# A 31-tap depthwise filter split into two phases, its gate taken from PSUM on VectorE, and a bias added as a matrix product

## The chip, the cores and the metric

One core of one Trainium2 chip. The metric is the time of one execution on the device in microseconds (us), the median over runs. The profile is one further execution, recorded by the hardware profiler; engines are TensorE (PE, its weight loads PEld), VectorE (DVE), ScalarE (ACT), GpSimd (POOL) and SyncE (SP, which here only issues DMAs).

## The reference

A backbone trunk with two layers over 1280 tokens (256 of context, 1024 latent) of 1024 channels. The first layer's mixer is a convolution module, and the change lies there:

```python
def conv_module(h, pw1_w, pw1_b, dw_w, dw_b, ln_g, ln_b, pw2_w, pw2_b):
    a, g = jnp.split(h @ pw1_w + pw1_b, 2, axis=-1)
    u = a * jax.nn.sigmoid(g)
    u = lax.conv_general_dilated(u, dw_w[:, None, :], window_strides=(1,),
                                 padding=[(CONV_PAD, CONV_PAD)], ...,
                                 feature_group_count=d) + dw_b      # 31 taps for each channel
    u = jax.nn.silu(layernorm(u, ln_g, ln_b))
    return u @ pw2_w + pw2_b
```

Context and latent tokens are filtered apart, each with zeros around it. Every sub-layer is modulated by rows of `silu(c) @ ada_w + ada_b` (6 x 1024 columns for each layer, for two vectors c). After the mixer come a mixture of experts, then a gated linear attention layer and a second mixture of experts. All of it is fp32.

## The kernel before

The program is a row of stages with a barrier between them. The stage of the change is `conv_taps`. It goes over the 1024 output channels in 8 chunks of 128 (channels on partitions, tokens along the columns).

Every fp32 product is made of three: weights and activations are split into a high half (`hi`, fp32r) and what is left (`lo`), and `product3` adds hi x hi, hi x lo, lo x hi. For each chunk SyncE loads the weights of both halves of `pw1` (`raw`, two buffers), ScalarE makes the high half (L577), GpSimd the low half (L477, 128 x 2048). TensorE makes three groups of tokens (0: 256 context tokens, 1 and 2: 512 latent tokens each) into PSUM: `zg` for the gate and `za` for the value, 48 matmuls for each group. ScalarE writes sigmoid(zg + bias) to `sg` (L601) and za + bias to `u` (L603); GpSimd multiplies them in place (L485). `u` has two buffers with zero columns between context and latent tokens.

VectorE then makes the 31 taps of the chunk over all 1295 columns: two scalar multiplies (L646, L648), 29 fused multiply-adds alternating between two accumulators (L653), and one sum of the two (L657) into `vt`, which the next stage reads. Before a chunk it copies that chunk's column of taps and biases to `vec` (L628). ScalarE's sigmoids of chunk n wait until the taps of chunk n-2 are summed.

In the same stage TensorE works off 20 units of modulation rows: 2 x 512 columns each, 64 matmuls with two stationary columns, in four strips of the array (L554). A unit's weights are two loads of 1 MB (`ada_w`), one buffer each, so a load waits until TensorE has used the half before it. There are five units for two chunks: three behind the even chunk, two behind the odd one. ScalarE takes the sums from PSUM (L588), GpSimd adds the bias, which SyncE has loaded (L498), and stores the two rows (L502).

Waits are written by hand with semaphores; the loops over pairs of chunks are hardware loops, with the first pair (and VectorE's last) written out.

Of the kernel before, what the change touches and what calls it, by code (L numbers as in the profile page):

```python
# [5 lines left out]
F32 = mybir.dt.float32  # L6
# [4 lines left out]
ALU = mybir.AluOpType  # L11
# [3 lines left out]
P = 128  # L15
# [373 lines left out]
STRIP = 32  # L389


def conv_taps(nc, d, ht, vt, vecs, cs):
# [3 lines left out]
    with ExitStack() as ctx:  # L396
# [5 lines left out]
        ada_b = ph.sb("ada_b", [P, P])  # L402
        ada_sum = ph.sb("ada_sum", [P, P])
        ada_row = ph.sb("ada_row", [P, P])
# [3 lines left out]
        vec = [ph.sb(f"vec{b}", [P, VEC_ROWS]) for b in range(2)]  # L408
        sg = [ph.sb(f"sg{g}", [P, N]) for g in range(3)]
        u = [ph.sb(f"u{b}", [P, CONV_W]) for b in range(2)]  # L410
        acc = [ph.sb(f"acc{b}", [P, CONV_OUT]) for b in range(2)]
# [3 lines left out]
        pairs = KC // 2  # L415

        with nc.Block() as block:
            @block.sync
            def _(sp):
                sp.dma_start(ident[:, :], d.ident).then_inc(s("rows_loaded"), 16)  # L420
                for r0, src in ((0, d.dw_w), (V_DWB, d.dw_b), (V_LNG, d.ln_g), (V_LNB, d.ln_b)):
                    n = src.shape[0]
                    sp.dma_start(rows[r0:r0 + n, :], src).then_inc(s("rows_loaded"), 16)
                sp.dma_start(rows[V_BA:V_BG + 1, :], d.pw1_b.rearrange("o (h n) -> (o h) n", h=2))\
                    .then_inc(s("rows_loaded"), 16)

                def load(b, i):
                    for h in range(2):
                        src = d.pw1_w[:, ds((i * 2 + b) * P + h * D, P)].rearrange("(k p) n -> p k n", p=P)
                        sp.dma_start(raw[b][:, :, h, :], src).then_inc(s(f"w_loaded{b}"), 16)  # L430

                def load_unit(j, i, first):
                    _, l, per, at, c0 = ADA_UNITS[j]
                    u = i * len(ADA_UNITS) + j
                    col = (i * per + at) * N + c0
                    for h in range(2):
                        if not (first and j == 0):

                            sp.wait_ge(s(f"ada_used{h}"), u)
                        half = slice(h * (KC // 2), (h + 1) * (KC // 2))  # L440
                        sp.dma_start(ada_w[h][:, :, :], d.ada_w[l, :, ds(col, N)]
                                     .rearrange("(p k) n -> p k n", k=KC)[:, half, :]).then_inc(s(f"ada_loaded{h}"), 16)
                    if not (first and j == 0):
                        sp.wait_ge(s("ada_out"), u)
                    else:
                        sp.wait_ge(s("ada_b_zero"), 1)
                    for st in (LAT, CTX):
                        sp.dma_start(ada_b[st:st + 3 * STRIP + 1:STRIP, :],
                                     d.ada_b[l, ds(col, N)].rearrange("(j n) -> j n", n=P))\
                            .then_inc(s("ada_b_loaded"), 16)  # L450

                def pair(i, first, last):
                    for b in range(2):
                        for j, unit in enumerate(ADA_UNITS):
                            if unit[0] == b:
                                load_unit(j, i, first)
                        if not last:

                            sp.wait_ge(s(f"w_lo{b}"), i + 1)
                            load(b, i + 1)  # L460

                for b in range(2):
                    load(b, 0)
                pair(0, True, False)
                with sp.Fori(1, pairs - 1) as i:
                    pair(i, False, False)
                pair(pairs - 1, False, True)

            @block.gpsimd
            def _(pool):  # L470
                pool.memset(ada_b[:, :], 0.0).then_inc(s("ada_b_zero"), 1)
                for b in range(2):
                    pool.memset(u[b][:, :], 0.0).then_inc(s("u_zero"), 1)

                def low(b, i):
                    pool.wait_ge(s(f"w_hi{b}"), i + 1)
                    pool.tensor_tensor(w.lo[:, :, :, :], raw[b][:, :, :, :], w.hi[:, :, :, :].bitcast(F32),  # L477
                                       ALU.subtract).then_inc(s(f"w_lo{b}"), 1)

                def gate(b, i):  # L480

                    for g, (t0, n, c0) in enumerate(CONV_GROUPS):
                        pool.wait_ge(s(f"sig_ready{g}{b}"), i + 1)
                        pool.wait_ge(s(f"a_ready{g}{b}"), i + 1)
                        pool.tensor_tensor(u[b][:, c0:c0 + n], u[b][:, c0:c0 + n], sg[g][:, 0:n], ALU.mult)\  # L485
                            .then_inc(s(f"u_ready{g}{b}"), 1)

                def units_out(b, i, first):

                    for j, (when, l, per, at, c0) in enumerate(ADA_UNITS):  # L490
                        if when != b:
                            continue
                        u = i * len(ADA_UNITS) + j
                        pool.wait_ge(s("ada_b_loaded"), (u + 1) * 32)
                        pool.wait_ge(s("ada_taken"), u + 1)
                        if not (first and j == 0):
                            pool.wait_ge(s("stored"), u * 32)
                        pool.tensor_tensor(ada_row[:, :], ada_sum[:, :], ada_b[:, :], ALU.add)\  # L498
                            .then_inc(s("ada_out"), 1)
                        pool.wait_ge(s("ada_out"), u + 1)  # L500
                        for st in (LAT, CTX):
                            pool.dma_start(d.mods[l].rearrange("s m n -> s (m n)")[st, ds((i * per + at) * N + c0, N)]  # L502
                                           .rearrange("(j n) -> j n", n=P),
                                           ada_row[st:st + 3 * STRIP + 1:STRIP, :]).then_inc(s("stored"), 16)

                low(0, 0)
                gate(0, 0)
                low(1, 0)
                units_out(0, 0, True)
                gate(1, 0)  # L510
                with pool.Fori(1, pairs) as i:
                    low(0, i)
                    units_out(1, i - 1, False)
                    gate(0, i)
                    low(1, i)
                    units_out(0, i, False)
                    gate(1, i)
                units_out(1, pairs - 1, False)
                pool.wait_ge(s("stored"), 32 * pairs * len(ADA_UNITS))

            @block.tensor
            def _(pe):
                pe.wait_ge(s("rows_loaded"), 96)
                pe.wait_ge(s("ada_acc_zero"), 1)
# [4 lines left out]
                def chunk(b, i, first):  # L529
                    pe.wait_ge(s(f"w_lo{b}"), i + 1)  # L530
                    for g, (t0, n, _) in enumerate(CONV_GROUPS):

                        if not (first and b == 0):
                            pe.wait_ge(s(f"a_ready{g}{1 - b}"), i + b)
                        for h, z in ((1, zg[g]), (0, za[g])):
                            for k in range(KC):
                                last = product3(pe, z[:, 0:n], w.hi[:, k, h, :], w.lo[:, k, h, :],
                                                ht.hi[:, k, t0:t0 + n], ht.lo[:, k, t0:t0 + n], k == 0, k == KC - 1)
                        last.then_inc(s(f"z_ready{g}{b}"), 1)

                def units(b, i, first):
                    for j, unit in enumerate(ADA_UNITS):
                        if unit[0] != b:
                            continue
                        u = i * len(ADA_UNITS) + j
                        if not (first and j == 0):

                            pe.wait_ge(s("ada_taken"), u)
                        for h in range(2):
                            pe.wait_ge(s(f"ada_loaded{h}"), (u + 1) * 16)  # L550
                            for k in range(KC // 2):
                                for j4 in range(N // P):

                                    last = pe.matmul(ada_acc[j4 * STRIP:j4 * STRIP + 2, 0:P],  # L554
                                                     cs[:, h * (KC // 2) + k, :], ada_w[h][:, k, j4 * P:(j4 + 1) * P],
                                                     start=h == 0 and k == 0, stop=h == 1 and k == KC // 2 - 1)
                            last.then_inc(s(f"ada_used{h}"), 1)

                for b in range(2):
# [2035 lines left out]
```

## Time and profile before

| | |
|---|---|
| Median of 3 runs | 3328.24 us (3327.05 to 3329.19) |
| Profiled execution | 3323.5 us, span 3321.9 us |
| Granted TensorE clock, mean | 0.867 of full speed |
| Filter stage | 118.2 to 588.5 us of the span |
| VectorE's taps | 169.39 to 588.45 us, 8 chunks |

The span is from the first to the last instruction. An engine's busy time leaves waiting out. A line such as L653 is a line of the kernel; an operation made in a loop or a helper has one line for all its instances. In a timeline, consecutive instructions of one line stand merged as one row with their count, so the row's duration is that of all of them.

### The profile page before, as it was taken

How to read it: one execution, taken by the hardware profiler on the slowest of the kernel's cores; microseconds unless marked ns; L12 is line 12 of the kernel's file. 1: busy time of each engine (PE TensorE's matmuls, PEld its weight loads, DVE VectorE, ACT ScalarE, POOL GpSimd, SP SyncE). 2: the span in 40 equal slices, each digit the busy share in tenths (PEclk: the TensorE clock that was granted, in tenths of full speed). 3: DMA queues.
4: the chain of work that ended last, by engine and by line, in shares of the span. 5: the costliest groups of instructions: out<-in, count | busy, mean ns of one | idle time of the engine just before them, and what ended most of it. 6: DMA issues, size and time to landing. Idle time of an engine off the chain costs nothing. (4 is left out here: it accounts for less than half of the span.)

```text
span 3321.9 us, 40914 instructions
## 1 busy us (share of the span) xinstructions
PE 2565.6 (77%) x13098; PEld 2050.7 (62%) x13098; DVE 2097.9 (63%) x1722; ACT 1406.0 (42%) x1455; POOL 512.9 (15%) x499
## 2 busy tenths in 40 slices
PE   4587770595399999999933998978494499999980
PEld 1466660484278888888832886757473388888860
DVE  2399999455476767588526001338554588888865
ACT  0211110443166666577523112434322277777752
POOL 0133320100000010001033000045200101001004
PEclk7688885796599999999965999989796699999995
DMA  8244330224188889799654211013454499999965
GB/s 301 92 153 153 126 107 20 96 76 172 42 322 311 322 320 327 280 349 385 264 219 172 100 48 52 20 53 109 172 194 147 153 376 382 393 383 391 394 254 215
DMA packets 297755, 701.18 MB, mean 211 GB/s; under 512 B 22640, under 2 KB 50096, under 8 KB 297654
## 3 DMA queue, kind: packets, MB, share of 16 engines
q1 hardware_dynamic: 259082, 570.79, 47.5%
q0 software_dynamic: 22656, 75.60, 6.4%
q10 hardware_dynamic: 15936, 53.75, 4.3%
q8 instruction: 47, 0.77, 0.1%
q14 instruction: 34, 0.28, 0.0%
HBM read 610.05 MB, written 91.06 MB: 211 GB/s over the span
## 5 line engine op out<-in xcount | busy, mean ns | idle before, releaser
L1394 DVE TENSOR_TENSOR moe_w_lo<-moe_w_raw,moe_w_hi 128x2048 fp32r<-128x2048 f32 x384 | 862.0, 2286 | 83.8 <-ACT moe_w_hi L1323 48.7
L1323 ACT ACTIVATE moe_w_hi<-moe_w_raw 128x2048 fp32r<-128x2048 f32 x384 | 714.8, 1909 | 63.9 <-issue 37.6
L653 DVE SCALAR_TENSOR_TENSOR taps_acc<-taps_u,taps_vec,taps_acc 128x1295 f32<-128x1295 f32 x232 | 387.2, 1744 | 0.0
L98 PE MATMUL moe_pg<-moe_w_hi,moe_xt_hi 128*128 128x512 f32 x592 | 243.8, 412 | 11.2 <-DVE moe_xt_lo L1405 5.9
L98 PE MATMUL moe_py<-moe_w_hi,moe_at_hi 128*128 128x512 f32 x592 | 241.6, 408 | 11.9 <-DVE moe_w_lo L1394 8.2
L99 PE MATMUL moe_pg<-moe_w_lo,moe_xt_hi 128*128 128x512 f32 x592 | 237.0, 400 | 0.0
L100 PE MATMUL moe_pg<-moe_w_hi,moe_xt_lo 128*128 128x512 f32 x592 | 236.8, 400 | 0.0
L99 PE MATMUL moe_py<-moe_w_lo,moe_at_hi 128*128 128x512 f32 x592 | 235.2, 397 | 0.0
L100 PE MATMUL moe_py<-moe_w_hi,moe_at_lo 128*128 128x512 f32 x592 | 234.8, 397 | 0.0
L100 PE MATMUL moe_pu<-moe_w_hi,moe_xt_lo 128*128 128x512 f32 x592 | 234.3, 396 | 0.0
L98 PE MATMUL moe_pu<-moe_w_hi,moe_xt_hi 128*128 128x512 f32 x592 | 234.1, 396 | 0.0
L99 PE MATMUL moe_pu<-moe_w_lo,moe_xt_hi 128*128 128x512 f32 x592 | 234.1, 396 | 0.0
L1226 POOL COPY moe_idx<-plan_token 128x1 int32 (+1 forms) x76 | 16.0, 210 | 1076.6 <-PE moe_pxt L1264 1076.5
L1440 DVE TENSOR_TENSOR moe_a<-moe_sil,moe_pu 128x512 f32<-128x512 f32 x74 | 50.9, 688 | 180.5 <-issue 130.4
L364 PE MATMUL norm_pt<-norm_ident,norm_h 128*128 128x128 f32 x224 | 55.1, 427 | 119.3 <-DVE norm_h L334 119.3
L1333 ACT ACTIVATE moe_y<-moe_py 128x1024 f32<-128x1024 f32 x74 | 76.0, 1027 | 146.1 <-PE moe_py L100 146.1
L98 PEld LDWEIGHTS moe_pg<-moe_w_hi,moe_xt_hi 128*128 128x128 f32 x592 | 113.4, 192 | 36.3 <-issue 12.4
L98 PEld LDWEIGHTS moe_py<-moe_w_hi,moe_at_hi 128*128 128x128 f32 x592 | 112.2, 190 | 35.8 <-issue 12.3
L1232 POOL DMA_INDIRECT moe_xg<-scratch_experts_in,moe_idx x76 | 115.0, 1514 | 123.4 <-issue 123.4
L1348 ACT ACTIVATE moe_xt_hi<-moe_pxt 128x1024 fp32r<-128x1024 f32 x74 | 75.8, 1024 | 129.4 <-PE moe_pxt L1264 129.4
L98 PE MATMUL glav_acc<-glav_w_hi,ht_next_hi 128*128 128x512 f32 x288 | 114.9, 399 | 20.0 <-DVE glav_w_lo L1738 20.0
L100 PEld LDWEIGHTS moe_pg<-moe_w_hi,moe_xt_lo 128*128 128x128 f32 x592 | 113.2, 191 | 27.4
(305 smaller groups left out, 5366.0 us busy)
## 6 DMA issues: line engine op xcount, KB each, us to landing
moe_w_raw<-in_moe_w SPq DMA_DIRECT2D x384, 1024.0 KB, 12.6
taps_ada_w<-in_ada_w SPq DMA_DIRECT2D x40, 1024.0 KB, 7.0
scratch_experts_out<-moe_y ACTq DMA_DIRECT2D x57, 512.0 KB, 6.4
norm_x<-scratch_residual SPq DMA_DIRECT2D x28, 512.0 KB, 3.3
scan_v<-scratch_gla_values SPq DMA_DIRECT2D x20, 512.0 KB, 4.0
scratch_experts_in<-norm_h POOLq DMA_DIRECT2D x18, 512.0 KB, 3.0
comb_x<-scratch_residual SPq DMA_DIRECT2D x18, 512.0 KB, 6.9
ada_w<-in_ada_w SPq DMA_DIRECT2D x4, 2048.0 KB, 28.0
```

The source lines that it names most:

```text
L98: pe.matmul(out, xh, wh, start=start, stop=False)
L99: pe.matmul(out, xh, wl, start=False, stop=False)
L100: return pe.matmul(out, xl, wh, start=False, stop=stop)
L364: last = pe.transpose(pt[b][:, k, :], h[b][:, k * P:(k + 1) * P], ident[:, :])
L653: dve.scalar_tensor_tensor(acc[q][:, :], u[b][:, k:k + CONV_OUT], vec[b][:, k:k + 1], acc[q][:, :], ALU.mult, ALU.add).then_inc(s(f"tap{q} ...
L1226: pool.tensor_copy(idx[:, :], plan.token[:, ds(k, 1)]).then_inc(s("idx_ready"), 1)
L1232: pool.indirect_dma_start(xg[0:rows, :], None, d.hd[:, :], bass.IndirectOffsetOnAxis(idx[0:rows, :], 0))\
L1323: act.activation(hi[m][:, cut, :], raw[m][p][:, cut, :], ACT.Copy).then_inc(s(f"{m}_hi{h}"), 1)
L1333: act.activation(y[:, :], py[:, :], ACT.Copy).then_inc(s("y_out"), 1)
L1348: act.activation(xt_hi[:, :, :], pxt[:, :, :], ACT.Copy).then_inc(s("xt_hi"), 1)
L1394: dve.tensor_tensor(lo[m][:, cut, :], raw[m][p][:, cut, :], hi[m][:, cut, :].bitcast(F32), ALU.subtract).then_inc(s(f"{m}_lo{h}"), 1)
L1440: dve.tensor_tensor(a[:, :], sil[:, :], pu[:, :], ALU.mult).then_inc(s("a_ready"), 1)
```

## The change

- **Filter.** The padded columns of `u` are stored as two phases (even and odd columns, 664 each; the zero columns become 16 and 32, so that both phases start alike, and the output has 1298 columns). With u0, u1 the phases and w the taps, one sum is shared: S = sum over j of (w[2j] + w[2j+1]) u1[j], 16 half-length taps. The even outputs are S + sum of w[2j] (u0 - u1)[j], 16 taps on `back`; the odd outputs are S + sum of w[2j+1] (u0 shifted by one - u1)[j], 15 taps on `ahead`. So 47 taps of 649 columns take the place of 31 of 1295, and there are two subtractions and two joins, which write every second column of `vt`. The summed taps (`both`) are made once.
- **Gate.** VectorE reads `za` from PSUM and does (za + bias) * sg in one instruction for each group, writing the two phases. ScalarE's L603 and GpSimd's L485 go. Gate n+1 stands on VectorE between the even and the odd half of chunk n. TensorE's groups of the next chunk wait for it (`u_ready`), since `za` and `zg` have one buffer for each group.
- **Modulation bias.** Four matmuls with one row (`one` x `ada_b`) start each unit's sums; GpSimd's L498 and `ada_sum` go, ScalarE writes one of five `ada_row` buffers, and GpSimd only issues the stores.
- **Order.** Units stand behind single groups (after groups 0, 1, 2 in even chunks, after 1 and 2 in odd ones; the first chunk keeps all three behind group 2). GpSimd makes the low half of chunk n+1 ahead of the stores of chunk n's units. The per-chunk vector copies go. The hardware loops over pairs become plain written-out code.

```diff
-GAP = PAD + CTX_LEN + PAD
-CONV_GROUPS = [(0, CTX_LEN, PAD), (CTX_LEN, N, GAP), (CTX_LEN + N, N, GAP + N)]
-CONV_W = GAP + SEQ + PAD
-CONV_OUT = GAP + SEQ - PAD
+LEAD = PAD + 1
+GAP = LEAD + CTX_LEN + LEAD
+CONV_GROUPS = [(0, CTX_LEN, LEAD), (CTX_LEN, N, GAP), (CTX_LEN + N, N, GAP + N)]
+CONV_W = GAP + SEQ + LEAD
+CONV_OUT = CONV_W - 2 * PAD
...
+EVEN, ODD = (TAPS + 1) // 2, TAPS // 2
+HALF_OUT = CONV_OUT // 2
...
+        def units_behind(n, g):
+            units = units_of(n)
+            if n == 0:
+                return units if g == 2 else []
+            return units[g:g + 1] if len(units) == 3 else units[g - 1:g] if g else []
...
             @block.gpsimd
+                low(0)
+                for n in range(KC):
+                    if n + 1 < KC:
+                        low(n + 1)
+                    for at in units_of(n):
...
+                        pool.wait_ge(s("ada_taken"), at + 1)
                         for st in (LAT, CTX):
+                            pool.dma_start(..., ada_row[j][st:st + 3 * STRIP + 1:STRIP, :]).then_inc(s(f"stored{j}"), 16)
...
             @block.tensor
+                def unit(at):
...
+                    for j4 in range(N // P):
+                        pe.matmul(ada_acc[j4 * STRIP:j4 * STRIP + 2, 0:P], one[:, :], ada_b[:, j4 * P:(j4 + 1) * P],
+                                  start=True, stop=False)
...
+                for n in range(KC):
+                    pe.wait_ge(s("w_lo"), n + 1)
+                    for g, (t0, m, _) in enumerate(CONV_GROUPS):
+                        if n:
+                            pe.wait_ge(s(f"sig_ready{g}"), n)
+                            pe.wait_ge(s(f"u_ready{g}"), n)
                         for h, z in ((1, zg[g]), (0, za[g])):
...
+                        last.then_inc(s(f"z_ready{g}"), 1)
+                        for at in units_behind(n, g):
+                            unit(at)
...
             @block.scalar
+                        act.activation(sg[g][:, 0:m], zg[g][:, 0:m], ACT.Sigmoid, bias=vecs[:, n, V_BG:V_BG + 1])\
+                            .then_inc(s(f"sig_ready{g}"), 1)
+                        if g == 2 and n + 1 < KC:
+                            high(n + 1)
+                        for at in units_behind(n, g):
+                            take(at)
...
             @block.vector
+                def gate(n):
+                    for g, (t0, m, c0) in enumerate(CONV_GROUPS):
+                        dve.wait_ge(s(f"z_ready{g}"), n + 1)
+                        dve.wait_ge(s(f"sig_ready{g}"), n + 1)
+                        dve.scalar_tensor_tensor(
+                            u[n % 2][:, :, c0 // 2:(c0 + m) // 2].rearrange("p q m -> p m q"),
+                            za[g][:, 0:m].rearrange("p (m q) -> p m q", q=2), vecs[:, n, V_BA:V_BA + 1],
+                            sg[g][:, 0:m].rearrange("p (m q) -> p m q", q=2), ALU.add, ALU.mult)\
+                            .then_inc(s(f"u_ready{g}"), 1)
...
+                gate(0)
+                for n in range(KC):
+                    for g in range(3):
+                        dve.wait_ge(s(f"u_ready{g}"), n + 1)
+                    if n:
+                        dve.wait_ge(s("odd_done"), n)
+                    dve.tensor_tensor(back[:, :], u[n % 2][:, 0, :], u[n % 2][:, 1, :], ALU.subtract)\
+                        .then_inc(s("back"), 1)
+                    shared(n, 0)
+                    dve.tensor_tensor(ahead[:, :], u[n % 2][:, 0, 1:], u[n % 2][:, 1, 0:CONV_W // 2 - 1], ALU.subtract)\
+                        .then_inc(s("ahead"), 1)
+                    even(n, 0)
+                    for j in range(1, EVEN):
+                        shared(n, j)
+                        even(n, j)
+                    join(n, 0, "even_done", 0)
+                    if n + 1 < KC:
+                        gate(n + 1)
+                    dve.wait_ge(s("even_done"), n + 1)
+                    for j in range(ODD):
+                        odd(n, j)
+                    join(n, 1, "odd_done", 1)
```

`shared`, `even` and `odd` are one instruction each: a scalar multiply where they begin a sum (shared 0, even 0 with the filter's bias, odd 1 with the bias), otherwise a fused multiply-add into one of the two accumulators, after a wait for the one before on that accumulator. `join` waits for both and adds them into every second column of `vt`.

## Rows read from the trace of the kernel before

**Rows 1.** The page, busy us of an engine, share of the span, instructions.

```profile
PE 2565.6 (77%) x13098; PEld 2050.7 (62%) x13098; DVE 2097.9 (63%) x1722; ACT 1406.0 (42%) x1455; POOL 512.9 (15%) x499
```

**Rows 2.** Windows: length, busy PE, PEld, DVE, ACT, POOL, clock, DMA share, GB/s.

```profile
276.00:330.00 54.00, 47.69 (x372) 39.99 (x373) 53.97 (x34) 5.89 (x10) 19.87 (x13) 0.86 0.46 153
...
545.00:592.00 47.00, 0.00 (x0) 0.00 (x0) 43.47 (x31) 0.00 (x0) 0.00 (x0) 0.50 0.01 4
```

**Rows 3.** Waits, 118 to 592 us: who waited for whom, total, times, longest.

```profile
ACT taps_sg L601 <- DVE taps_vec L628: 90.1, 4, 30.4
...
PE taps_ada_acc L554 <- DMA taps_ada_w<-in_ada_w: 70.7, 23, 10.9
DVE taps_acc L646 <- POOL taps_u L485: 39.9, 1, 39.9
```

**Rows 4.** Timeline of VectorE: start, duration, line, operation, tiles, count.

```profile
169.39 0.95 DVE L646 TENSOR_SCALAR taps_acc<-taps_u,taps_vec 128x1295 f32<-128x1295 f32 x1 [39.91 <-POOL taps_u L485]
...
335.26 49.90 DVE L653 SCALAR_TENSOR_TENSOR taps_acc<-taps_u,taps_vec,taps_acc 128x1295 f32<-128x1295 f32 x29
...
542.28 0.95 DVE L646 TENSOR_SCALAR taps_acc<-taps_u,taps_vec 128x1295 f32<-128x1295 f32 x1
543.15 0.89 DVE L648 TENSOR_SCALAR taps_acc<-taps_u,taps_vec 128x1295 f32<-128x1295 f32 x1
543.96 42.95 DVE L653 SCALAR_TENSOR_TENSOR taps_acc<-taps_u,taps_vec,taps_acc 128x1295 f32<-128x1295 f32 x29
586.94 1.51 DVE L657 TENSOR_TENSOR taps_out<-taps_acc 128x1295 f32<-128x1295 f32 x1
```

**Rows 5.** Groups of VectorE by line and shape: busy us, mean ns, idle before.

```profile
L653 DVE SCALAR_TENSOR_TENSOR taps_acc<-taps_u,taps_vec,taps_acc 128x1295 f32<-128x1295 f32 x29 | 42.9, 1559 | 0.0
...
L2258 DVE SCALAR_TENSOR_TENSOR scan_state<-scan_state,scan_fall,scan_pds 128x256 f32<-128x256 f32 x80 | 33.2, 476 | 45.7 <-PE scan_pds L2113 45.7
...
L991 DVE COPY route_lg<-route_pt 128x256 f32<-128x256 f32 x1 | 0.4, 424 | 0.0
```

**Rows 6.** Timeline of VectorE in the attention scan, four fused operations.

```profile
2226.94 1.64 DVE L2258 SCALAR_TENSOR_TENSOR scan_state<-scan_state,scan_fall,scan_pds 128x256 f32<-128x256 f32 x4
```

**Rows 7.** Timeline of GpSimd and VectorE where a low half meets taps.

```profile
350.79 5.76 POOL L477 TENSOR_TENSOR taps_w_lo<-taps_raw,taps_w_hi 128x2048 fp32r<-128x2048 f32 x1
...
401.88 5.09 POOL L477 TENSOR_TENSOR taps_w_lo<-taps_raw,taps_w_hi 128x2048 fp32r<-128x2048 f32 x1 [0.64 <-ACT taps_w_hi L577]
...
402.53 5.81 DVE L653 SCALAR_TENSOR_TENSOR taps_acc<-taps_u,taps_vec,taps_acc 128x1295 f32<-128x1295 f32 x1
```

**Rows 8.** Timeline of ScalarE, chunks 0 and 1; a sigmoid starts when its group ends.

```profile
166.75 0.69 ACT L601 ACTIVATE taps_sg<-taps_zg,taps_vec 128x512 f32<-128x512 f32 x1 [9.61 <-PE taps_za L100]
...
167.90 1.91 ACT L577 ACTIVATE taps_w_hi<-taps_raw 128x2048 fp32r<-128x2048 f32 x1
169.70 0.28 ACT L588 ACTIVATE taps_ada_sum<-taps_ada_acc 128x128 f32<-128x128 f32 x1
...
186.69 0.28 ACT L588 ACTIVATE taps_ada_sum<-taps_ada_acc 128x128 f32<-128x128 f32 x1 [8.80 <-PE taps_ada_acc L554]
193.47 0.48 ACT L601 ACTIVATE taps_sg<-taps_zg,taps_vec 128x256 f32<-128x256 f32 x1 [6.50 <-PE taps_za L100]
...
204.33 0.69 ACT L601 ACTIVATE taps_sg<-taps_zg,taps_vec 128x512 f32<-128x512 f32 x1 [10.02 <-PE taps_za L100]
```

**Rows 9.** Windows around a group of 512 columns and around two units.

```profile
193.00:204.30 11.30, 11.30 (x53) 9.41 (x52) 11.30 (x8) 0.84 (x2) 1.25 (x1) 1.00 0.07 24
...
169.70:177.50 7.80, 3.73 (x64) 2.04 (x64) 7.80 (x4) 0.28 (x2) 7.18 (x4) 0.61 0.67 245
...
398.80:402.00 3.20, 1.77 (x64) 1.42 (x56) 3.20 (x3) 3.17 (x4) 1.21 (x2) 1.00 0.26 65
```

**Rows 10.** DMA issues of the page: count, KB each, median us to landing.

```profile
taps_ada_w<-in_ada_w SPq DMA_DIRECT2D x40, 1024.0 KB, 7.0
```

More of the change, by code:

```diff
@@ L401, in conv_taps @@
         ada_w = [ph.sb(f"ada_w{h}", [P, KC // 2, N]) for h in range(2)]
-        ada_b = ph.sb("ada_b", [P, P])
-        ada_sum = ph.sb("ada_sum", [P, P])
-        ada_row = ph.sb("ada_row", [P, P])
+        ada_b = ph.sb("ada_b", [1, N])
+        one = ph.sb("one", [1, 2])
+        ada_row = [ph.sb(f"ada_row{j}", [P, P]) for j in range(len(ADA_UNITS))]
         ada_acc = ph.ps("ada_acc", [P, N])
@@ L452, in pair @@
[L452 to L466, printed above, removed]
@@ L467, in _ @@
-                pair(pairs - 1, False, True)
+                        if h == 0:
+                            sp.dma_start(ada_b[:, :], d.ada_b[layer:layer + 1, col:col + N])\
+                                .then_inc(s("ada_b_loaded"), 16)
+                for n in range(2):
+                    load(n)
+                for n in range(KC):
+                    for at in units_of(n):
+                        load_unit(at)
+                    if n + 2 < KC:
+                        load(n + 2)
@@ L480, in gate @@
[L480 to L500, printed above, removed]
+                    pool.memset(u[b][:, :, :], 0.0).then_inc(s("u_zero"), 1)
@@ L508, in _ @@
[L508 to L519, printed above, removed]
+                                           ada_row[j][st:st + 3 * STRIP + 1:STRIP, :]).then_inc(s(f"stored{j}"), 16)
@@ L521, in _ @@
+                for j in range(per_pair):
+                    pool.wait_ge(s(f"stored{j}"), 32 * (total // per_pair))
             @block.tensor
@@ L539, in chunk @@
[L539 to L557, printed above, removed]
@@ L559, in _ @@
-                for b in range(2):
-                    chunk(b, 0, True)
-                    units(b, 0, True)
-                with pe.Fori(1, pairs) as i:
-                    for b in range(2):
-                        chunk(b, i, False)
-                        units(b, i, False)
+                                last = product3(pe, z[:, 0:m], w.hi[:, k, h, :], w.lo[:, k, h, :],
+                                                ht.hi[:, k, t0:t0 + m], ht.lo[:, k, t0:t0 + m], k == 0, k == KC - 1)
@@ L660, in _ @@
-                vector(0, 0)
-                for b in range(2):
-                    chunk(b, 0, first=True)
-                with dve.Fori(1, pairs - 1) as i:
-                    for b in range(2):
-                        chunk(b, i)
-                for b in range(2):
-                    chunk(b, pairs - 1, last=True)
-                dve.wait_ge(s("taps_summed"), KC)
+                dve.tensor_tensor(both[:, :, 0:ODD], vecs[:, :, 0:2 * ODD:2], vecs[:, :, 1:2 * ODD:2], ALU.add)\
+                    .then_inc(s("both_ready"), 1)
```

213 lines of the change are left out of this document (106 added, 107 removed).

## The prediction

> **What bounds the kernel now.** The page comes first: over the whole span VectorE is busy 63% and TensorE 77% [rows 1]. These are averages over stages with different limits; the edit lies in one stage, the filter stage, from 118.2 to 588.5 us. So I cut that stretch into windows [rows 2]. VectorE is busy through the whole of the middle window and nearly all of the last, while TensorE, at 47.69 of 54 us in the middle, does nothing in the last: the taps set the end. The waits of the stage say the same from the other side [rows 3]: the sigmoids wait 90.1 us for VectorE (through the vector copy), VectorE itself waits once, 39.9 us, at the start, for the first gated chunk. TensorE's 70.7 us of waiting for modulation weights is hidden behind VectorE, but it must be kept in mind for a change that makes VectorE quicker.
>
> Then the timeline of VectorE [rows 4]. Taps run from 169.39 to 586.94 + 1.51 = 588.45 us, 419.1 us for 8 chunks. The last chunk has GpSimd idle: 29 fused taps in 42.95 us, so one every 1.481 us. Its duration is 1559 ns for 1295 columns and that of the fused operation of 256 columns 476 ns [rows 5]: 1083 / 1039 = 1.042 ns a column. 1295 columns are then 1.349 us, and 0.132 us of the spacing is fixed. A chunk with GpSimd at work takes 49.90 us for the same 29: 6.95 us lost.
>
> **The new VectorE chunk.** Half a chunk's output is 649 columns. I need the fixed part at a short length: four fused operations of 256 take 1.64 us in all with 0.476 for the last [rows 5, 6], so one starts every 0.388 us, 0.267 of it elements and 0.121 fixed. The fixed part doesn't shrink with length. I take 0.13: 0.676 + 0.13 = 0.806 us per fused half-length tap.
> - Even half: 30 fused taps 24.2; two scalar multiplies, which go at two elements per cycle (1295 start to start in 0.81, of which 0.675 are elements [rows 4]), 0.47 and 0.54; two subtractions of 664 and 663 at 0.77; the join 0.76 (its row is 1.51 for 1295 [rows 4], 0.16 fixed, less 0.08 of overlap with the next); 0.3 where an operation waits for the one just before it. Sum 27.8 us.
> - Odd half: 14 fused 11.3, one scalar multiply 0.54, join 0.76, 0.2 for waits: 12.8 us.
> - Gate, new on VectorE: 256 + 512 + 512 columns out of PSUM, 1.33 + 3 x 0.13 = 1.7 us. The 256-column row reads PSUM too and has no extra [rows 5].
>
> Taps are then 40.6 us a chunk against 46.2 before (542.28 to 588.45). A quarter of the multiplications goes (47 x 649 against 31 x 1295 elements), an eighth of the time, because 31 fixed parts and one join become 51 and more.
>
> **GpSimd.** A fused tap has two SBUF inputs. The one that met a low half took 5.81 us where 1.56 is usual [rows 7]: 4.25 us lost, for a low half of 5.09 us in all. That stays, 7 times. The gates and bias sums on GpSimd go; with them 6.95 - 4.25 = 2.7 us a chunk. The gate on VectorE has one SBUF input. The Trainium skill's page "SBUF — State Buffer", section "Who interferes with whom", calls this an exclusive lock held for the whole instruction, against VectorE operations with two SBUF inputs. The row of 5.81 agrees, and by that rule the new gate would be free of it; my sum puts no loss on it either way.
>
> So a steady chunk is 27.8 + 1.7 + 12.8 + 4.25 = 46.6 us; before, 46.2 + 7.0 = 53.2 (the chunk of the 49.90).
>
> **The new wait.** VectorE runs in order, and gate(n+1) stands between the halves of chunk n. In chunk 0 it comes too early. Chunk 0's third group ends at 166.75 as now [rows 8]; sigmoid and gate bring VectorE's start to 168.1 (169.39 before, since the identity pass on ScalarE and GpSimd's multiply are gone). Even half plus the low half of chunk 1: 168.1 + 27.8 + 4.25 = 200.2. TensorE still makes three modulation units back to back behind chunk 0, limited by their 1 MB loads (7.0 us each [rows 10]), to 186.7; then group 0 by 193.5, group 1 by 204.3 [rows 8]. Now one unit stands before group 2: 1.77 us of matmul at clock 1.00 [rows 9], and 0.1 for its four bias products. Group 2, 10.9 us like group 1, ends at 217.2, sigmoid 217.9, gate 218.6. VectorE stands for about 17 us, and behind it the odd half.
>
> From there: 218.6 + 12.8 + 6 x 46.6 + 40.6 = 551.6 us. The stage ends 36.9 us earlier. Other edits I cost at nothing: the bias load and products (TensorE has spare time), 8 vector copies of 0.2 on VectorE that go (inside the 0.3s), two small operations on the summed taps (VectorE idle before 168), the unrolled loops. Without TensorE's cover the bias products would be 20 x 0.1 = 2 us. The stores of the modulation rows stay on GpSimd's queue behind the next low half; the row they wait for is in its own buffer, and only the unit five later needs it.
>
> **Does TensorE keep up?** Chunk n+2 may start when gate(n+1) has read PSUM and the low half is there: sigmoid 0.7, high half 1.9, low half up to 5.8 after group 2 [rows 7, 8], 8.4 us. Groups take 7, 10.9 and 10.9 (group 0 has half the columns of group 1 and yet took 193.47 - 186.69 = 6.8 us: it starts at the lower clock), units inside 1.9 each [rows 8, 9]. With two inside that is 8.4 + 28.8 + 3.8 = 41.0 us from group 2 to group 2. 41.0 is below 46.6. Released by the gate instead, it delivers 0.4 + 28.8 + 3.8 + 0.7 = 33.7 us after it. At gate(2): VectorE gets there at 218.6 + 12.8 + 27.8 + 4.25 = 263.5; TensorE has it at 217.2 + 41.0 + 0.7 = 258.9. A unit's two loads, 7 us each and overlapping, lie behind a group of 10.9 us, or behind the wait for the low half.
>
> **Strided places.** The gate writes the two phases alternately, the joins every second column. The nearest row is the reordering copy with a source step of 8 columns: 424 ns for 256 [rows 5], which is 0.267 of elements and the same 0.16 fixed as the join. I take no extra; the other bound is double time for the five operations of a chunk, 2.7 us. The Trainium skill ("Advanced Engine Details and Errata", "SBUF Cachelines") speaks against the change here: full rate wants two hits on a 16-byte line, and the gate's alternating writes have none in a row. By it the time would be rival C's; the reordering copy's row doesn't bear it out, but that one reads PSUM.
>
> **Rivals.**
> - A, the forecast: VectorE bounds after one stall. 0.71. Its own range 3284 to 3307: fixed part between 0.12 and 0.16 for some 55 operations in each of 8 chunks (-4 to +13 us), the stall 14 to 19 us.
> - B, units keep waiting for loads inside a chunk (8.5 us each, as (186.69 - 169.70) / 2 now). Three-unit chunks then need 8.4 + 28.8 + 17 = 54.2 us from group 2 to group 2. Gate 2 is 8.6 us late (217.2 + 54.2 + 0.7 against 263.5), gates 4 and 6 each 54.2 + 45.7 - 2 x 46.6 = 6.7: +22, 3313. For it: 70.7 us of waits now. Against: now they are back to back. 0.11.
> - C, strided writes at half rate: 8 x 1.35 for joins and 6 x 1.33 for gates, +19: 3310. 0.10.
> - D, the slower side: TensorE's clock. It now pauses in each chunk and runs thin unit matmuls between groups; the granted clock was 0.61 in a unit that waited for its weights [rows 9]. If it stayed at the lower level (1.2 GHz) for all of the groups, 28.8 becomes some 55 and the loop 67 us: 6 x 20 us lost, 3413. It decides against the change from a loop of 46.6 + 37/6 = 52.8 us. Against: group 1 runs at 1.00 behind a group 0 that starts low [rows 9]. 0.04.
> - Better than A (low halves falling into VectorE's waits, 4.25 us each, three or four times): 3275. 0.04.
>
> **Numbers.** The profiled execution took 3323.5 us, its span 3321.9; the median of the three is 3328.24, 0.14% more. The difference is taken from the median: 3328.2 - 36.9 = 3291.3. The range must leave out D and part of the tails: 3279 to 3313. A measurement tells about 0.2%, 7 us. Faster: A, B, C and the better case, 0.94; within: 0.02; slower: 0.04.
>
> **What would show it.** The half-length fused tap: duration near 0.88 us, one per 0.806. The first chunk: VectorE idle 17 us before a gate, and no long wait at later gates. One tap a chunk stretched by 4.2 us. TensorE waits for the gates, not the other way round. Taps end near 552. The prediction is wrong if the wait before gates repeats (B or D), if gate or join durations are twice their element time (C), or if the fixed part grows with the two chains now one tap of 0.8 us apart.

## The result and the profile after

| | before | after |
|---|---|---|
| Median of 4 runs | 3328.72 us (3327.05 to 3330.28) | 3291.57 us (3288.28 to 3293.28) |
| Profiled execution | 3323.5 us, span 3321.9 | 3288.3 us, span 3286.7 |
| Granted TensorE clock, mean | 0.867 | 0.876 |
| Filter stage | 118.24 to 588.45, 470.2 us | 120.39 to 554.38, 434.0 us |

The ratio is 0.989 (0.9877 to 0.9902): the changed kernel is 37 us faster, and 3291.3 was forecast. The filter stage is 36.2 us shorter; the forecast had 36.9.

The page first, which answers to [rows 1]: busy time of each engine over the span.

```profile
PE 2559.9 (78%) x13258; PEld 2053.7 (62%) x13258; DVE 2053.0 (62%) x1892; ACT 1393.6 (42%) x1431; POOL 462.6 (14%) x455
```

It says little, as before. The stage says more. Groups of the stage by line and form (count | busy us, mean ns of one | idle before and what ended it):

```profile
L614 DVE SCALAR_TENSOR_TENSOR taps_acc<-taps_back,channel_vectors,taps_acc 128x649 f32<-128x649 f32 x120 | 107.0, 892 | 0.0
L602 DVE SCALAR_TENSOR_TENSOR taps_acc<-taps_u,taps_both,taps_acc 128x649 f32<-128x649 f32 x120 | 107.0, 891 | 0.0
L629 DVE SCALAR_TENSOR_TENSOR taps_acc<-taps_ahead,channel_vectors,taps_acc 128x649 f32<-128x649 f32 x112 | 91.4, 890 | 0.0
...
L484 POOL TENSOR_TENSOR taps_w_lo<-taps_raw,taps_w_hi 128x2048 fp32r<-128x2048 f32 x8 | 58.0, 7255 | 248.0 <-ACT taps_w_hi L552 248.0
...
L636 DVE TENSOR_TENSOR taps_out<-taps_acc 128x649 f32<-128x649 f32 x16 | 33.9, 2118 | 1.1
...
L589 DVE SCALAR_TENSOR_TENSOR taps_u<-taps_za,channel_vectors,taps_sg 128x512 f32<-128x512 f32 x16 | 16.8, 1112 | 33.8 <-ACT taps_sg L567 33.8
...
L589 DVE SCALAR_TENSOR_TENSOR taps_u<-taps_za,channel_vectors,taps_sg 128x256 f32<-128x256 f32 x8 | 5.2, 656 | 15.6 <-ACT taps_sg L567 15.6
```

Three things are to be seen. The half-length tap takes 890 ns whatever it reads, as forecast (0.88). The gate's 512 columns take 1112 ns. And GpSimd's low half, 5.09 us in [rows 7], is 7.3 us on average.

VectorE's timeline of one steady chunk and of the last one (start, us for the row; rows of several instructions are merged):

```profile
237.42 0.84 DVE L650 TENSOR_TENSOR taps_ahead<-taps_u 128x663 f32<-128x663 f32 x1
238.18 0.61 DVE L610 TENSOR_SCALAR taps_acc<-taps_back,channel_vectors 128x649 f32<-128x649 f32 x1
238.71 0.89 DVE L602 SCALAR_TENSOR_TENSOR taps_acc<-taps_u,taps_both,taps_acc 128x649 f32<-128x649 f32 x1
239.51 0.89 DVE L614 SCALAR_TENSOR_TENSOR taps_acc<-taps_back,channel_vectors,taps_acc 128x649 f32<-128x649 f32 x1
...
262.06 0.89 DVE L614 SCALAR_TENSOR_TENSOR taps_acc<-taps_back,channel_vectors,taps_acc 128x649 f32<-128x649 f32 x1
263.06 4.94 DVE L636 TENSOR_TENSOR taps_out<-taps_acc 128x649 f32<-128x649 f32 x1
267.91 2.55 DVE L589 SCALAR_TENSOR_TENSOR taps_u<-taps_za,channel_vectors,taps_sg 128x256 f32<-128x256 f32 x3
270.30 0.87 DVE L629 SCALAR_TENSOR_TENSOR taps_acc<-taps_ahead,channel_vectors,taps_acc 128x649 f32<-128x649 f32 x1
...
283.16 0.85 DVE L647 TENSOR_TENSOR taps_back<-taps_u 128x664 f32<-128x664 f32 x1
...
310.02 4.94 DVE L636 TENSOR_TENSOR taps_out<-taps_acc 128x649 f32<-128x649 f32 x1
...
513.90 0.85 DVE L647 TENSOR_TENSOR taps_back<-taps_u 128x664 f32<-128x664 f32 x1
...
553.55 0.83 DVE L636 TENSOR_TENSOR taps_out<-taps_acc 128x649 f32<-128x649 f32 x1
```

Thirty fused taps start from 238.71 to 262.06, one every 0.805 us. From join to join it is 310.02 - 263.06 = 46.96 us (46.6 forecast). The stretched instruction is the join, not a tap: 4.94 us against 0.83. The last chunk runs from 513.90 to 554.38, 40.5 us (40.6 forecast). In the kernel before, the chunks between the first and the last two take 53.3 us on average (227.00 to 493.53 for five); this is 47.0 in their place.

GpSimd's low halves in the same view:

```profile
219.87 4.48 POOL L484 TENSOR_TENSOR taps_w_lo<-taps_raw,taps_w_hi 128x2048 fp32r<-128x2048 f32 x1 [30.97 <-ACT taps_w_hi L552]
261.09 6.21 POOL L484 TENSOR_TENSOR taps_w_lo<-taps_raw,taps_w_hi 128x2048 fp32r<-128x2048 f32 x1 [34.51 <-ACT taps_w_hi L552]
303.01 11.26 POOL L484 TENSOR_TENSOR taps_w_lo<-taps_raw,taps_w_hi 128x2048 fp32r<-128x2048 f32 x1 [32.37 <-ACT taps_w_hi L552]
```

Each of the last two ends 0.7 us before the stretched join does (267.30 against 268.00, 314.27 against 314.96). The third began 303.01, 7.0 us before the join of 310.02, and VectorE's taps in between went at their usual spacing: GpSimd stood, and VectorE lost nothing until the join.

The wait in chunk 0, on VectorE:

```profile
201.77 0.84 DVE L636 TENSOR_TENSOR taps_out<-taps_acc 128x649 f32<-128x649 f32 x1
202.52 0.69 DVE L589 SCALAR_TENSOR_TENSOR taps_u<-taps_za,channel_vectors,taps_sg 128x256 f32<-128x256 f32 x1
204.80 1.13 DVE L589 SCALAR_TENSOR_TENSOR taps_u<-taps_za,channel_vectors,taps_sg 128x512 f32<-128x512 f32 x1 [1.59 <-ACT taps_sg L567]
218.08 1.17 DVE L589 SCALAR_TENSOR_TENSOR taps_u<-taps_za,channel_vectors,taps_sg 128x512 f32<-128x512 f32 x1 [12.15 <-ACT taps_sg L567]
219.08 0.87 DVE L629 SCALAR_TENSOR_TENSOR taps_acc<-taps_ahead,channel_vectors,taps_acc 128x649 f32<-128x649 f32 x1
```

From 202.52 to 219.08 VectorE does 3 us of gates and stands for 13.7 us. Later gates have no wait: three in 2.55 us at 267.91. The waits of the stage confirm it (us in total, times, longest):

```profile
PE taps_zg L99 <- DVE taps_u L589: 53.5, 5, 13.1
DVE taps_u L589 <- ACT taps_sg L567: 49.4, 5, 15.6
```

TensorE now waits for the gates, up to 13.1 us at a time. VectorE's 49.4 us are these 13.7 and the wait for the very first groups.

### The profile page after: what moved, and what is told of

It is laid out like the page before. It is cut to its first block and busy times, and to the rows that moved or that the text cites. A ratio compares the mean times of both kernels' runs of the same rounds, so it can differ in the third digit from the quotient of the medians.

```text
span 3286.7 us, 41009 instructions
## 1 busy us (share of the span) xinstructions
PE 2559.9 (78%) x13258; PEld 2053.7 (62%) x13258; DVE 2053.0 (62%) x1892; ACT 1393.6 (42%) x1431; POOL 462.6 (14%) x455
## 5 line engine op out<-in xcount | busy, mean ns | idle before, releaser
L567 ACT ACTIVATE taps_sg<-taps_zg,channel_vectors 128x512 f32<-128x512 f32 (+1 forms) x24 | 14.8, 616 | 290.6 <-PE taps_za L101 290.6
```

Of the source, the lines that this page charges most:

```text
L567: act.activation(sg[g][:, 0:m], zg[g][:, 0:m], ACT.Sigmoid, bias=vecs[:, n, V_BG:V_BG + 1])\
```

## Experiments

The ratios are against the kernel before, run on the same chip. The changed kernel's own ratio, 0.989, is the other mark. The length of the filter stage in the one profiled execution stands beside them (before 470.2 us, changed 434.0); the time outside the stage was 2850 to 2859 us in the ten profiles, so the stage tells small differences better than the medians do.

**The filter alone.** The kernel before with nothing but the two-phase filter (VectorE's loop over pairs of chunks is written out with it); the phases are read in place out of `u` with a step of 2, and gates, bias sums, units and low halves stay where they were.

```diff
+                    src, tap = u[n % 2][:, 1 + 2 * j:1 + 2 * j + 2 * HALF_OUT - 1:2], both[:, n, j:j + 1]
...
+                    dve.tensor_tensor(back[:, :], u[b][:, 0:CONV_W:2], u[b][:, 1:CONV_W:2], ALU.subtract)\
+                        .then_inc(s("back"), 1)
```

> The kernel before with the two-phase filter alone: gate, low halves, bias and units as before, VectorE reads u in place with a step of two columns. Theory (the halved taps are the gain): VectorE's chunk is 40.6 us of taps plus the 6.95 us that GpSimd took before, 47.5 us; the first chunk starts at the old 169.4 and there is no wait in chunk 0, so the taps end near 540 and the time is 3279 to 3283 us, 8 to 12 below the changed kernel. Rival (GpSimd is held off): in the changed kernel's trace the low half took up to 11.3 us from start to end, because it got the port only at a join; here three gates and a low half of every chunk have to get in between the short taps, the gated chunk comes late, VectorE waits for it, and the time is 3295 to 3312 us. Rival (stepped reads are slow): a tap of the shared sum takes over 1.2 us instead of 0.89, and the time is over 3330 us.

Measured: 3282.93 us, ratio 0.987 (0.9854 to 0.9887), 8.6 us below the changed kernel (7 by the two ratios, whose intervals overlap), and inside the expected 3279 to 3283. The stage is 428.1 us, 5.9 shorter than in the changed kernel. The filter makes all of the gain, and what was added to it gains nothing or takes some back. Its taps by line, then GpSimd's and VectorE's operations in the timeline:

```profile
L646 DVE SCALAR_TENSOR_TENSOR taps_acc<-taps_u,taps_both,taps_acc 128x649 f32<-128x649 f32 x120 | 106.5, 888 | 0.0
```

```profile
277.63 20.98 POOL L504 TENSOR_TENSOR taps_ada_row<-taps_ada_sum,taps_ada_b 128x128 f32<-128x128 f32 x1 [5.98 <-ACT taps_ada_sum L594]
...
308.16 6.24 POOL L491 TENSOR_TENSOR taps_u<-taps_u,taps_sg 128x512 f32<-128x512 f32 x1 [5.73 <-ACT taps_u L609]
314.36 5.10 POOL L483 TENSOR_TENSOR taps_w_lo<-taps_raw,taps_w_hi 128x2048 fp32r<-128x2048 f32 x1
...
371.15 0.88 POOL L504 TENSOR_TENSOR taps_ada_row<-taps_ada_sum,taps_ada_b 128x128 f32<-128x128 f32 x1 [5.14 <-ACT taps_ada_sum L594]
```

```profile
298.40 0.91 DVE L680 TENSOR_TENSOR taps_out<-taps_acc 128x649 f32<-128x649 f32 x1
...
313.30 1.79 DVE L680 TENSOR_TENSOR taps_out<-taps_acc 128x649 f32<-128x649 f32 x1
315.01 4.49 DVE L638 COPY taps_vec<-channel_vectors 128x36 f32<-128x36 f32 x1
```

The taps of L646 read with a step of 2 and take 888 ns, no more than contiguous ones. GpSimd's gate of 512 columns is held as well (1.09 us in the kernel before at 400.15, 6.24 here), until VectorE's join at 313.30; the low half behind it then goes straight through, and VectorE's small copy (0.18 us elsewhere) takes 4.49 beside it. The longest wait is that of a bias sum of 128 columns, 0.5 us of work: 20.98 us, until the join at 298.40.

**The rest alone.** The changed kernel with 31 full-length taps; gate n+1 stands behind tap 20 of chunk n.

```diff
-                    dve.tensor_tensor(back[:, :], u[n % 2][:, 0, :], u[n % 2][:, 1, :], ALU.subtract)\
-                        .then_inc(s("back"), 1)
...
+                    for k in range(TAPS):
+                        if k == CUT and n + 1 < KC:
+                            gate(n + 1)
+                        tap(n, k)
```

> The changed kernel with the 31 full-length taps back (gate from PSUM on VectorE after tap 20, bias as a product, units between groups, all kept). Theory: taps 46.2 us a chunk, gate 1.7 us as its writes are contiguous here, low half 4.25 us, and a wait of about 16 us in chunk 0; the taps then end some 7 us later than in the kernel before, 3336 us: the rest of the change alone loses. Rival: taking the gates off GpSimd and the units apart is worth its 2.7 us a chunk and more, 3310 us, so that the filter is only half of the gain.

Measured: 3331.43 us, ratio 1.0008 (0.9998 to 1.0017): no difference (stage 471.0 us against 470.2). My 3336 was 5 us too high, the rival's 3310 falls. VectorE and GpSimd in a steady chunk:

```profile
323.15 1.79 DVE L583 SCALAR_TENSOR_TENSOR taps_u<-taps_za,channel_vectors,taps_sg 128x256 f32<-128x256 f32 x3
324.86 5.58 DVE L600 SCALAR_TENSOR_TENSOR taps_acc<-taps_u,channel_vectors,taps_acc 128x1298 f32<-128x1298 f32 x2
```

```profile
311.71 15.89 POOL L481 TENSOR_TENSOR taps_w_lo<-taps_raw,taps_w_hi 128x2048 fp32r<-128x2048 f32 x1 [31.41 <-ACT taps_w_hi L549]
```

The low half is held from 311.71 until the gates at 323.15. It ends 4.45 us after they begin, so part of it lies beside the gates, which it does not slow: they take 1.79 us with this contiguous write. Two taps then take 5.58 where 3.04 is usual, 2.5 us lost instead of 4.25. The chunk is 343.81 - 293.16 = 50.65 us from join to join, against 53.3. Five such chunks save 13.3 us, and chunk 6 (48.1 us against 48.75) 0.6; chunk 0, with 3.13 + 12.54 us of idle, takes 72.5 us (171.66 to 244.16) against 57.6 (169.39 to 227.00), 14.9 more, and eats all of it. The run holds the gate on VectorE, the bias as a product and the order of the units together; no run takes one of them alone.

**The gate's write.** The gate writes each phase contiguously and reads its inputs with a step of 2.

```diff
-                            u[n % 2][:, :, c0 // 2:(c0 + m) // 2].rearrange("p q m -> p m q"),
-                            za[g][:, 0:m].rearrange("p (m q) -> p m q", q=2), vecs[:, n, V_BA:V_BA + 1],
-                            sg[g][:, 0:m].rearrange("p (m q) -> p m q", q=2), ALU.add, ALU.mult)\
+                            u[n % 2][:, :, c0 // 2:(c0 + m) // 2],
+                            za[g][:, 0:m].rearrange("p (m q) -> p q m", q=2), vecs[:, n, V_BA:V_BA + 1],
+                            sg[g][:, 0:m].rearrange("p (m q) -> p q m", q=2), ALU.add, ALU.mult)\
```

> The changed kernel with the gate going phase by phase: it writes each phase contiguously and reads PSUM and the sigmoid with a step of two. In the changed kernel the gate of 512 columns takes 1.14 us where a fused operation of that size would take 0.74, and a join that writes with a step of two takes no extra. Theory (the alternating writes cost it): 0.74 and 0.48 us, three gates 1.7 instead of 2.4 us, 4 to 5 us less in all: 3287 us. Rival (it is the read of PSUM beside a read of SBUF at this width, or the stepped read costs the same): durations stay at 1.1 us, 3291.6 us; if stepped PSUM reads are slower still, above it.

Measured: 3290.72 us, ratio 0.9887 (0.987 to 0.9903). The gate falls from 1112 to 740 ns (512 columns) and from 656 to 474 (256), and the steady chunk from 46.96 to 46.3 us. The stage is 3.8 us shorter in the profiled execution (430.2), while the medians differ by 0.9, less than runs can tell. With full-length taps, where the gate reads and writes contiguously, it takes 0.75 us for 512 columns too, so neither the read of PSUM nor its step of 2 costs anything. So the alternating write is the cause of the longer gate; its effect on the time is too small to be shown by the medians.

**Units from chunk 1 on.** No modulation unit behind chunk 0, one behind each group from chunk 1 until all 20 are done.

```diff
-            units = units_of(n)
-            if n == 0:
-                return units if g == 2 else []
-            return units[g:g + 1] if len(units) == 3 else units[g - 1:g] if g else []
+            at = (n - 1) * 3 + g
+            return [at] if 0 <= at < total else []
```

> The changed kernel with no modulation unit behind chunk 0 and one behind every group from chunk 1 on (20 units over 21 places). Theory: group 2 of chunk 1 is ready near 209 instead of 217.3, VectorE's wait in chunk 0 is 8 to 9 us shorter and nothing else waits, since TensorE needs 41 to 43 us from chunk to chunk and VectorE 47: 3283 us. Rival: with three units in every chunk TensorE becomes the bound (loads of 2 MB behind a group of 256 columns): VectorE waits at later gates and the time is 3291 us or more.

Measured: 3284.86 us, ratio 0.9876 (0.9859 to 0.9892), 6.7 below the changed kernel (stage 428.6 us, 5.4 shorter). VectorE's gates of chunk 0:

```profile
203.55 1.64 DVE L586 SCALAR_TENSOR_TENSOR taps_u<-taps_za,channel_vectors,taps_sg 128x256 f32<-128x256 f32 x2
212.72 1.18 DVE L586 SCALAR_TENSOR_TENSOR taps_u<-taps_za,channel_vectors,taps_sg 128x512 f32<-128x512 f32 x1 [7.53 <-ACT taps_sg L564]
```

The wait is 7.5 us instead of 13.7, and no later gate waits. Six of the 13.7 us come from the units behind chunk 0. What is left is the time TensorE takes for the three groups and the two units now between them. I had expected 8 to 9 us: group 0 of chunk 1, for which TensorE now waits idle until the low half is there, took 8.3 us at a granted clock of 0.68, where it took 5.9 at 1.00 in the changed kernel's profile.

**All units behind group 2.** The other order, with the loads' waits in one place.

```diff
-            if n == 0:
-                return units if g == 2 else []
-            return units[g:g + 1] if len(units) == 3 else units[g - 1:g] if g else []
+            return units if g == 2 else []
```

> The changed kernel with all units of a chunk behind its last group, as in the kernel before. Their weights are then waited for, 8 to 9 us each, and three units take some 19 us behind group 2. Theory: from group 2 to group 2 TensorE needs 19 + 28.8 = 48 us behind a three-unit chunk and 40 behind a two-unit one, but it is ready 9 us before VectorE asks, so the slack takes it: 3289 to 3292 us, as the changed kernel. Rival (the interleaving carries part of the gain): VectorE waits for group 2 at three or more gates, 3300 us or more.

Measured: 3291.72 us, ratio 0.9891 (0.9875 to 0.9908), stage 435.1 us, as the changed kernel. TensorE's waits for DMAs:

```profile
PE taps_ada_acc L515 <- DMA taps_ada_b<-in_ada_b: 40.2, 12, 4.2
...
PE taps_ada_acc L522 <- DMA taps_ada_w<-in_ada_w: 14.1, 12, 2.4
```

TensorE waits 54 us for loads here and loses nothing, because VectorE still sets the pace. Interleaving the units buys nothing in this kernel. It does take the waits away: in the changed kernel TensorE waits 8.0 us for loads in all, the whole of it behind chunk 0, where rival B needed 8.5 us at each unit.

**Low halves on VectorE.** GpSimd makes none; VectorE does, one instruction in the odd half of each chunk up to the sixth, and two ahead of them (the first before any gate, the second among the even taps of chunk 0).

```diff
+                        if j == 1 and n + 2 < KC:
+                            low(n + 2)
                         odd(n, j)
```

> The changed kernel with the low halves of the weights made by VectorE (one operation of 128 x 2048, 2.29 us elsewhere in the trace) in place of GpSimd, which then only issues stores. In the changed kernel each low half on GpSimd stretches one join from 0.84 to 4.94 us. Theory (VectorE pays for GpSimd's work by being locked out, and longer than its own operation takes): 4.1 - 2.2 = 1.9 us for each of 6 low halves behind the first wait, and 2.2 us at the start of the first chunk, together some 13 us: 3277 to 3280 us. Rival (VectorE is the bound and any work added to it is a loss): 15 us more, 3306 us. Second rival: TensorE gets the weights too late and the gates wait, 3290 us.

Measured: 3277.12 us, ratio 0.9847 (0.9831 to 0.9863), 14.5 below the changed kernel (stage 424.1 us, 9.9 shorter).

```profile
259.69 0.83 DVE L633 TENSOR_TENSOR taps_out<-taps_acc 128x649 f32<-128x649 f32 x1
260.44 2.50 DVE L581 SCALAR_TENSOR_TENSOR taps_u<-taps_za,channel_vectors,taps_sg 128x256 f32<-128x256 f32 x3
...
263.57 2.29 DVE L626 TENSOR_TENSOR taps_w_lo<-taps_raw,taps_w_hi 128x2048 fp32r<-128x2048 f32 x1
```

The join is back at 0.83 us. The low half costs VectorE 2.29 us as its own instruction (2.20 until the next one starts, at 265.77) and 4.1 as GpSimd's neighbour. In the profile five chunks of 45.0 us instead of 47.0 and 2.0 us in the odd half of chunk 0 make 11.7 us; gate(1) ended 1.8 us later, counted from the stage's start, behind a group 0 of chunk 1 that took 7.7 us at a granted clock of 0.74. The 2.2 us that I expected at the first chunk bring nothing, since VectorE stands for TensorE at gate(1) (18.4 us here). What the medians show beyond the stage's 9.9 us lies outside the stage and is not explained.

**All three together.** Low halves on VectorE, units from chunk 1 on, contiguous gate write.

> The changed kernel with three edits: low halves on VectorE, no units behind chunk 0 and one behind every group after it, the gate phase by phase. Theory: the gains add, 13 + 7 + 4 us, since VectorE still needs 44.5 us a chunk and TensorE 41 to 43: 3266 to 3270 us. Rival: with VectorE at 44.5 us TensorE's loop becomes the bound in part of the chunks, 3273 to 3280 us.

Measured: 3268.17 us (3265.77 to 3270.60), ratio 0.9818 (0.9802 to 0.9834), stage 410.7 us. The chunk is 298.17 - 253.75 = 44.4 us from join to join. This version is 23 us (0.7%) below the changed kernel and 60 us below the one before; it beats both. Whether low halves on VectorE would do as much for the filter alone, no run shows.

**GpSimd's low half beside the gates.** It stays on GpSimd, but waits for the first gate of the chunk, so that it overlaps instructions that it does not block.

```diff
                     pool.wait_ge(s("w_hi"), n + 1)
+                    if n:
+                        pool.wait_ge(s("u_ready0"), n)
```

> The changed kernel with one more wait: GpSimd starts the low half of chunk n+1 only when VectorE has done group 0 of gate n. The gate has one SBUF input, the taps have two. In the run with full-length taps the low halves began during a gate and a steady chunk lost only 2.5 us to each (50.65 against 48.1 us), where the changed kernel loses 4.1. Theory (only operations with two SBUF inputs are locked out): the low half runs beside groups 1 and 2 of the gate, some 1.8 us of it cost nothing, and the rest is taken from the first odd tap: no join of 4.94 us, an odd tap stretched by 2.3 to 2.8 us instead, six chunks 1.3 to 1.8 us shorter each, 3280 to 3284 us. Rival (the gate is locked out as well, or the low half doesn't get in between the groups): the stretched operation is a gate or again a join, and the time stays at 3291.6 us.

Measured: 3288.12 us, ratio 0.988 (0.9864 to 0.9897); 3.5 below the changed kernel, less than the medians can tell, and above my range. What is shown here is shown by the rows. VectorE, then GpSimd, at one gate:

```profile
264.83 0.83 DVE L638 TENSOR_TENSOR taps_out<-taps_acc 128x649 f32<-128x649 f32 x1
265.58 2.49 DVE L591 SCALAR_TENSOR_TENSOR taps_u<-taps_za,channel_vectors,taps_sg 128x256 f32<-128x256 f32 x3
267.92 3.66 DVE L631 SCALAR_TENSOR_TENSOR taps_acc<-taps_ahead,channel_vectors,taps_acc 128x649 f32<-128x649 f32 x1
```

```profile
266.39 4.50 POOL L486 TENSOR_TENSOR taps_w_lo<-taps_raw,taps_w_hi 128x2048 fp32r<-128x2048 f32 x1 [38.02 <-DVE taps_u L591]
312.00 4.50 POOL L486 TENSOR_TENSOR taps_w_lo<-taps_raw,taps_w_hi 128x2048 fp32r<-128x2048 f32 x1 [37.55 <-DVE taps_u L591]
```

The mechanism is there: the low half takes 4.50 us each time, the gates 2.49 beside it, join 0.83, and the next tap loses 2.8 instead of 4.1. The chunk is 45.6 us (low half to low half), 1.35 less, for five chunks 6.8. The profiled stage is only 3.4 us shorter, though, since its odd half of chunk 0 started 3.1 us later, counted from the stage's start. The windows over group 0 of chunk 1 show most of it (columns: us, then busy time of PE, PEld, DVE, ACT, POOL with instructions, granted clock, DMA share, GB/s); first the changed kernel, then this one:

```profile
187.20:193.10 5.90, 5.90 (x49) 5.89 (x50) 5.90 (x8) 0.28 (x1) 1.13 (x2) 1.00 1.07 372
```

```profile
187.15:194.90 7.75, 7.75 (x49) 7.74 (x50) 7.75 (x11) 0.28 (x2) 1.12 (x2) 0.74 0.84 293
```

The same 48-matmul group takes 1.85 us longer at a granted clock of 0.74 than at 1.00, in both kernels right behind units that wait for their loads; the other 1.2 us lie in the units' loads. Nothing in the edit touches either. The profiles of the other runs with the same three units in front show both: the group took 5.9 us at 1.00 in one more (the contiguous gate), and 7.4 to 7.8 us at 0.74 to 0.79 in three more (units behind group 2, full-length taps, low halves on VectorE). The changed kernel's own profile had the rarer, quicker case.

## Why the prediction was right

**VectorE bounds the stage, before and after.** Right. TensorE waits 53.5 us for gates in the changed kernel, and with all units behind group 2 TensorE waits 54 us for loads at no cost. Rival B falls, and D: the mean clock even rose, 0.867 to 0.876.

**The half-length tap, 0.806.** Right: 0.805. Both ways of the sum, the even half (26.9 us up to the join, 27.6 with it, against 27.8) and the odd half (12.86 against 12.8), hold.

**The low half, 4.25 us, once a chunk.** Right in size (4.94 - 0.83 = 4.1), wrong in place. I had it stretch a tap; it stretches a join, or a scalar multiply (4.80 and 4.84 us in chunk 0), and GpSimd waits for that moment. VectorE's loss is the same.

**The gate, 1.7 us.** Mis-sized. Three take 2.39 us (267.91 to 270.30). With a contiguous write they are back at 1.7. The forecast put no extra on strided places; of rival C's terms one, the alternating write, is real at 0.37 us per 512 columns. The other, the joins' step of 2, is nothing: 0.83 us for 649 columns, beside 0.85 for a contiguous subtraction of 664. Over six gates that is 4 us, not 19.

Of the Trainium skill's rule that full rate wants two hits on a 16-byte line ("Advanced Engine Details and Errata", "SBUF Cachelines") the runs bear out the order but not a threshold: the alternating write, with no two hits in a row, costs; the joins' write and the taps' read with a step of 8 bytes have two hits a line and cost nothing. By the rule only the gate's share of rival C was due, 6 x 1.33 = 8 of its 19 us; the prediction gave it the whole of C, joins included, and measured are 4.

**The wait in chunk 0.** Right in kind, 13.7 us instead of about 17. Counted from the stage's start, gate(1) ended 98.7 us in, against 100.4 forecast: group 0 took 5.9 us at clock 1.00, where I had 6.8 from a row at 0.87, and the unit loads were quicker by 1.6, offset by 0.4 in the group with a unit before it and 0.4 in the sigmoid and the gate. VectorE reached the gate at 202.5 - 120.4 = 82.1 against 200.2 - 118.2 = 82.0.

**The sum.** From the stage's start, gate(1) was 1.7 us early; from there to the end it is 554.38 - 219.08 = 335.3 us against 12.8 + 6 x 46.6 + 40.6 = 333.0, 2.3 late, the gates 4 us longer, the low halves and the even halves 2 shorter. So 434.0 stands against 433.4: two errors of some 2 us cancelled. The first was luck of this one profile, whose execution was also the fastest of the four: with group 0 at 7.4 to 7.8 us, as in four of the six profiles with these units in front, gate(1) would have ended about when forecast and the stage taken some 436 us, an estimate from those rows. The time outside the stage moved by 1 us between the profiled executions (stage -36.2, span -35.2), the 2.15 us by which the stage began later partly given back, and none of it was part of the argument.

**What I had not separated.** The forecast priced the change as a whole and never asked what each half was worth. The runs do: the filter alone -44 us (3282.9 against 3327.1), everything else alone 0, and everything else on top of the filter +7 to +9 (+5.9 in the stage). Its steady chunk is even 1 us shorter (47.0 us; the filter alone takes 48.0 on average, joins at 249.99 and 490.16 for five), but the mid-chunk gate makes VectorE stand 13.7 us once, and taking work off GpSimd doesn't free VectorE of the low half, the longest of GpSimd's operations.

## What to carry to other kernels

Price an operation by its element time and its fixed part apart: a quarter fewer multiplications gave an eighth less time here because each of 51 instructions, where there were 32, pays a fixed part (0.13 us for a fused tap), and two of them are the added subtractions. An in-order engine that takes a producer's step in the middle of its own loop waits once for the whole start-up of the pipeline; look at what stands before that step in the first iteration (moving three modulation units away from there cut the wait by 6 us). And where a helper engine's instruction blocks the bounding engine for longer than that engine would need for the work itself (4.1 against 2.2 us), give the work to the bounding engine.

## What the runs showed of the hardware that was not expected

- **GpSimd can be held for long.** Its 4.5 us subtraction took 6.2 to 11.3 us in the changed kernel and 11.4 to 15.9 with full-length taps, as long as VectorE issued fused taps back to back, and got in where a join, a scalar multiply or a gate came. The Trainium skill ("SBUF — State Buffer", "Who interferes with whom") has whoever issues first hold the shared pair for the whole instruction; these rows show in addition that a string of fused taps (each row overlapping the next by 0.08 us) can keep it for many instructions: eight at 303.01, and some 25 in the filter-alone kernel, where three bias sums of 128 columns took 18.6 to 21.0 us, each until a join. Why the low half of the kernel before got in within one tap [rows 7] stays open. There GpSimd had finished another operation 0.6 us earlier; in the filter-alone kernel the low halves that follow another GpSimd operation so closely are quick too (4.7 to 5.1 us), and it is a gate after an idle of 5.7 us that is held. The idle time alone doesn't decide it: the bias sum at 371.15, after 5.14 us of idle, got in at once (0.88 us; the tap at 371.63 took 1.09). No run separates the patterns.
- **The gate, with one of its two tensor inputs in PSUM, is not blocked.** Three take 2.49 us beside a running low half and 2.50 without. A single tensor input in SBUF is not what spares it: the scalar multiplies have one too and are stretched to 4.80 and 4.84 us in the changed kernel, and the copy of 36 columns to 4.49 in the filter-alone kernel.
- **Alternating writes between two rows cost 0.73 ns a column** ((1112 - 740) / 512 on 512 columns, 0.71 on 256), while step-2 reads and writes of fp32 cost nothing.
